# A two-layer encoder trunk on one core: the second layer's first projection taken from the unnormalised rows, and two steps of the feed-forward norm put in another order

## The chip, the cores and the metric

One core of one Trainium2 chip runs the whole kernel in one launch. The metric is the device time in microseconds (us) of that core. TensorE does the matmuls, VectorE (DVE in the rows) and ScalarE (ACT) the elementwise work, GpSimd (POOL) elementwise work beside them; SyncE (SP) issues every DMA.

## The reference, cut to what matters

The input is x (512 tokens by 1024 channels, float32) with a conditioning vector c. Two layers follow one another:

```
h   = modulated(LN(x))                 # scale and shift from c
z   = h @ w_in                         # 17 blocks of 128 columns
y   = four mixers(z) -> RMS per group -> @ w_out
x   = LN1(alpha * x + gate1 * y)
a   = conv3(modulated(x) @ w_up)       # 2 * 2816 columns, causal, width 3
x   = LN2(alpha * x + gate2 * ((val * silu(gate)) @ w_down))
```

The mixers are a gated MLP over 128 positions, latent attention, a diagonal state-space model (S5) and a gated linear recurrence (HGRN2). LN subtracts the mean over the 1024 channels and divides by the deviation.

## The kernel before

All activations lie channels by tokens: xa is 8 slices (k = 0 to 7) of 128 channels by 512 tokens and holds the residual stream, hm the modulated input. Weights come in chunks of 512 KB (128 by 1024) in a ring of 4 slots; SP loads a chunk when TensorE has begun one of the chunks before it (semaphore chunk_used). Every order is written out by hand, one list per engine, and semaphores tie the lists together.

There are five norms. Norm 1 is at the start; norms 2 and 4 stand between the output projection and the feed-forward part of layers 0 and 1; norm 3 stands between the layers and norm 5 at the end. A norm goes like this. VectorE adds each finished output bank to xa (residual, L1126) and adds up the slices (sum_x, L1134); ScalarE squares them (L1744); GpSimd adds the squares (L2078, L2210). TensorE multiplies the sums by a column of ones (norm_stats, L480: 32 records of 128x1). VectorE works out mean and variance on 4 columns (norm_var, L1069 to L1073), ScalarE the root (L1749), VectorE the reciprocal and the product mean * rstd (norm_rstd, L1078, L1080). TensorE spreads these two rows over the partitions (norm_spread, L475, 16 records) and VectorE applies them slice by slice (norm_apply: L1090 multiplies, L1096 subtracts). GpSimd then writes the modulated slice (modulate, L2090), and ScalarE turns xa into the next residual (affine, L1761).

In norms 2 and 4 the first block of w_up is already multiplied with the raw xa while the norm is worked out (raw_slice, L983, two records for a product). Since LN is linear in the rows but for mean and deviation, `up_raw` is put right afterwards: times the spread deviation, minus the column sums of the weighed weights times mean * rstd, plus a bias. The weights are weighed by weigh (L1648, two products), their column sums come from collect (L1654 to L1656, three additions of 1024, 512 and 256 columns with a wait after each of the first two) and from two small matmuls (L1000) before raw_slice(7). The other blocks of w_up are float32 matmuls in three parts (L460, L461, L462) from a high and a low half: ScalarE writes the high half of the weights (L1784), GpSimd the low half (weights_low, L2179), VectorE and GpSimd in turn the low half of the activations (h_low, L1669 for even k, L2219 for odd k). Blocks 1 and 2 go slice by slice with these (the pair loop), blocks 3 to 43 follow.

Between the layers (norm 3) there is no such raw product. TensorE does norm_pause: the sums, one filler matmul (keep_awake, L499), the spreads, two fillers. Then blocks CQ0 and CQ1 of w_in go slice by slice as hm comes in (L740), and CKV, F0, F1 and the rest follow by project (L551, two records for a product of 128x512), mixed with the mixers' small matmuls in a fixed order. At the same time VectorE goes from norm_apply straight to the mixers' tables: L1196 to L1202, then, after ScalarE's exponentials L1794 and L1795 (which stand behind the eight L1761), the S5 chain L1205 to L1326, and later the softmax of the attention (L1363), whose result TensorE turns at L713.

Of the kernel before, what the change touches and what calls it, by code (L numbers as in the profile page):

```python
# [13 lines left out]
P = 128  # L14
# [96 lines left out]
RAW_WEIGHED, RAW_SUM, RAW_UP, NRAW = 1, 2, 3, 3  # L111
# [28 lines left out]
def trunk(nc, x, consts, c_row, par_a, par_b, w_ada, w_in, w_out, w_up, w_down, out):  # L140
    ctx = ExitStack()
    with ctx:
# [128 lines left out]


# [4 lines left out]
        def sems(*names):  # L277
# [10 lines left out]
            **sems("silu_ready", "ada_used", "ln_par", "ln_sq", "ln_sumx", "ln_sumq", "ln_stat", "ln_var", "ln_sd",  # L288
                   "ln_rstd", "ln_bcast", "ln_normed", "ln_x", "ln_accx", "ln_accq", "h_par", "h_ready", "resid_mm", "resid"),
# [73 lines left out]
        def _(sp):  # L363
# [79 lines left out]
        def _(pe):  # L443
# [81 lines left out]
            last.then_inc(S["ln_accx"], 1)  # L525
# [5 lines left out]
            for l in range(L):  # L531

                def project(p, part):
# [15 lines left out]
                    else:  # L549
                        for k in ((0, 1, 2), (3, 4, 5), (6, 7))[part]:  # L550
                            last = mm(bank[:, :], w[:, k, :], hm[:, k, :], start=(k == 0), stop=(k == KD - 1))  # L551
                            if k == 0:
                                last.then_inc(S["chunk_used"], 2 if p == 2 else 1)
# [182 lines left out]
                w0, w1 = chunk(l, 0), chunk(l, 1)  # L736
                for k in range(KD):
                    pe.wait_ge(S["h_ready"], (2 * l) * KD + (k + 1))
                    for j, w in ((0, w0), (1, w1)):
                        last = mm(banks[2 + j][:, :], w[:, k, :], hm[:, k, :], start=(k == 0), stop=(k == KD - 1))  # L740
                        if k == 0 and j == 0:
# [265 lines left out]
                for k in range(KD):  # L1007
                    pe.wait_ge(S["h_lo_odd" if k % 2 else "h_lo"], l * (KD // 2) + k // 2 + 1)
                    for r, (w_hi, w_lo) in enumerate(pair):
# [4 lines left out]
                        if k == KD - 1:  # L1014
                            last.then_inc(S["up_mm"], 1)
                for m in range(3, 2 * KF):
# [38 lines left out]
                mm(banks[7][:, 63:64], ones, ones[:, 0:1], start=True, stop=True).then_inc(S["chunk_used"], TAIL - 1)  # L1055
                norm_pause(2 * l + 3, DOWN_DONE[-1])
# [3 lines left out]
        def _(v):  # L1060
# [21 lines left out]
            def norm_apply(n, low=None):  # L1082

                v.wait_ge(S["ln_bcast"], (n - 1) * 2 + 1)
                own = KD - SHARED if n == 2 * L + 1 else KD
                for k in range(own + (3 if low is not None else 1)):
                    if k == 5 and low is not None:
                        v.wait_ge(S["up_mm"], (n // 2 - 1) * (2 * KF) + 1)
                    if k < own:
                        ch.post(V.tensor_tensor(xa[:, k, :], xa[:, k, :], banks[0][:, :], ALU.mult))  # L1090
                    if k == 1:
                        v.wait_ge(S["ln_bcast"], (n - 1) * 2 + 2)
                    if 0 < k <= own:
                        if k == own:
                            ch.settle()
                        V.tensor_tensor(xa[:, k - 1, :], xa[:, k - 1, :], banks[1][:, :], ALU.subtract)\  # L1096
# [71 lines left out]
            v.wait_ge(S["silu_ready"], 1)  # L1168
# [17 lines left out]
            for l in range(L):  # L1186
# [486 lines left out]
                norm_rstd(2 * l + 2)  # L1673
                collect()
                norm_apply(2 * l + 2, h_low)

                v.wait_ge(S["up_mm"], l * (2 * KF) + 1)
# [48 lines left out]
                if l + 1 < L:  # L1726
                    modulated(l + 1, 0)
                for n, m in enumerate(DOWN_DONE):
                    residual(2 * l + 1, n, m, banks[m][:, :], g2p)
                    sum_x(2 * l + 1, n, DOWN_DONE)  # L1730
                norm(2 * l + 3)
                V.memset(small[:, 94:95], 0.0).then_inc(S["layer_done"], 1)
# [3 lines left out]
        def _(a):  # L1736
# [28 lines left out]
            A(silu_c[:, :], silu_c[:, :], ACT.Silu).then_inc(S["silu_ready"], 1)  # L1765
# [5 lines left out]
            a.wait_ge(S["ln_accx"], 1)  # L1771
# [14 lines left out]
            for l in range(L):  # L1786
# [21 lines left out]
                def evict(p):  # L1808
                    j = WIN[p]
                    a.wait_ge(S["proj_mm"], l * NPROJ + p + 1)  # L1810
                    bank = banks[2 + p] if p < 2 else banks[p % 2]
# [248 lines left out]
                if l + 1 == L:  # L2060
                    for r in range(2):
                        a.wait_ge(S["ln_bcast"], (2 * L) * 2 + 3 + r)
                        A(last_rows[:, r, :], banks[2 + r][:, :], ACT.Identity).then_inc(S["h_hi"], 1)
                affine(2 * l + 3, l + 1 < L)
# [3 lines left out]
        def _(g):  # L2068
# [28 lines left out]
            for l in range(L):  # L2097
# [123 lines left out]

                weights_low(KD + 3)
# [122 lines left out]
```

## Time and profile before

| | |
|---|---|
| median of 3 runs | 1423.6 us (1423.28 to 1427.83) |
| the profiled execution: its time, its span | 1428.15 us, 1426.4 us |
| TensorE busy | 1353.4 us, 95% of the span |
| VectorE, GpSimd, ScalarE busy | 785.5, 535.0, 506.2 us |
| mean granted TensorE clock | 0.966 of full |
| chain that ended last: TensorE, VectorE | 76%, 16% |

A busy TensorE is not one at its peak: a matmul's record overlaps the next one, and the rate is read from starts. Durations below are from this one execution.

### The profile page before, as it was taken

The page shows a single profiled execution, that of the slowest core. Times are in us where ns is not written, and L with a number is a line of the kernel's source. Part 1 is how long each engine was busy: PE and PEld are TensorE (multiplying, and loading weights), DVE is VectorE, ACT ScalarE, POOL GpSimd, SP SyncE. Part 2 cuts the span into 40 slices and gives each one's busy share as a digit, 9 for nine tenths or more (in the row PEclk, how much of TensorE's full clock was granted, in tenths as well). Part 3 has the DMA queues.
Part 4 walks back from the last instruction along what each step waited for, and adds up shares of the span by engine and source line. Part 5 has one row for each costly group of instructions (what it writes and reads, how often), then busy time and mean ns, then how long its engine had stood idle before and what let it go on. Part 6 is the DMA issues. An engine that isn't in the chain of part 4 may idle for free.

```text
span 1426.4 us, 17232 instructions
## 1 busy us (share of the span) xinstructions
PE 1353.4 (95%) x6868; PEld 1006.5 (71%) x6868; DVE 785.5 (55%) x1380; ACT 506.2 (35%) x766; POOL 535.0 (38%) x327
## 2 busy tenths in 40 slices
PE   6999999999999999899899999999999999989987
PEld 3445676786788888688665577677688888868866
DVE  5985778656776776432468656664743333321134
ACT  2523224335433333332242422442453333332223
POOL 0630100665444444344346110055644444434433
PEclk9998999999999999899999999999999999999998
DMA  9355733032555655454224451102133323223321
GB/s 385 146 118 163 170 121 100 16 103 89 188 196 190 188 182 180 160 178 161 106 72 112 84 74 37 45 17 84 49 103 98 95 89 102 90 74 89 97 66 60
DMA packets 64801, 166.79 MB, mean 117 GB/s; under 512 B 14288, under 2 KB 26960, under 8 KB 64208
## 3 DMA queue, kind: packets, MB, share of 16 engines
q1 hardware_dynamic: 64720, 165.68, 38.1%
q8 instruction: 55, 0.90, 0.2%
q14 instruction: 26, 0.21, 0.0%
HBM read 160.04 MB, written 5.62 MB: 116 GB/s over the span
## 4 chain that ended last, share of the span: by engine, by line
PE 76%; DVE 16%; issue 3%; DMA 2%; ACT 2%; POOL 1%; SPq 1%; ACTq 0%; POOLq 0%
PE bank L460 19%; PE bank L462 18%; PE bank L461 18%; PE bank L551 6%; PE bank L545 3%; PE bank L576 2%; PE bank L475 1%; DVE xa L1090 1%; DVE scr L1289 1%; PE bank L480 1%; DVE xa L1096 1%; PE bank L704 1%; PE bank L469 1%; DVE ada L1151 1%; DMA s_w<-scr 1%
## 5 line engine op out<-in xcount | busy, mean ns | idle before, releaser
L2179 POOL TENSOR_TENSOR ring_r<-ring,scr_r 128x1024 fp32r<-128x1024 f32 x146 | 352.8, 2418 | 450.0 <-ACT scr_r L1784 449.6
L460 PE MATMUL bank<-ym_r,scr_r 128*128 128x512 f32 x688 | 274.0, 398 | 5.2 <-DVE hm_r L1669 3.5
L462 PE MATMUL bank<-hm_r,scr_r 128*128 128x512 f32 x688 | 273.1, 397 | 0.0
L461 PE MATMUL bank<-ym_r,ring_r 128*128 128x512 f32 x688 | 270.4, 393 | 0.0
L460 PE MATMUL bank<-scr_r 128*128 128x512 f32 x480 | 196.8, 410 | 29.5 <-issue 14.2
L461 PE MATMUL bank<-scr_r,ring_r 128*128 128x512 f32 x480 | 191.0, 398 | 0.0
L1697 DVE SCALAR_TENSOR_TENSOR scr<-bank,pb,scr 128x511 f32<-128x511 f32 x86 | 64.5, 750 | 197.7 <-ACT scr L2035 197.6
L551 PE MATMUL bank<-hm,ring 128*128 128x512 f32 x352 | 171.0, 628 | 0.0
L1784 ACT ACTIVATE scr_r<-ring 128x1024 fp32r<-128x1024 f32 x146 | 152.7, 1047 | 39.9 <-DMA ring<-in_w_up 17.4
L1151 DVE SCALAR_TENSOR_TENSOR ada<-ada,silu_c 128x1024 f32<-128x1024 f32 x80 | 134.3, 1681 | 49.7 <-DMA ada<-in_w_ada 49.7
L460 PEld LDWEIGHTS bank<-ym_r,scr_r 128*128 128x128 f32 x688 | 129.3, 188 | 38.8 <-issue 5.1
L462 PEld LDWEIGHTS bank<-hm_r,scr_r 128*128 128x128 f32 x688 | 129.3, 188 | 32.2
L461 PEld LDWEIGHTS bank<-ym_r,ring_r 128*128 128x128 f32 x688 | 128.7, 187 | 32.3
L2035 ACT ACTIVATE scr<-bank,pb 128x512 f32<-128x512 f32 x86 | 66.7, 776 | 211.7 <-PE bank L462 211.7
L462 PE MATMUL bank<-scr_r 128*128 128x512 f32 x352 | 141.7, 403 | 0.0
L460 PEld LDWEIGHTS bank<-scr_r 128*128 128x128 f32 x480 | 92.7, 193 | 53.1 <-issue 16.3
L551 PEld LDWEIGHTS bank<-hm,ring 128*128 128x128 f32 x352 | 67.2, 200 | 73.2 <-issue 71.1
L461 PEld LDWEIGHTS bank<-scr_r,ring_r 128*128 128x128 f32 x480 | 92.9, 193 | 21.9
L1715 DVE TENSOR_TENSOR scr_r<-scr,scr_r 128x512 fp32r<-128x512 f32 x44 | 41.3, 939 | 121.5 <-ACT scr_r L2048 121.4
L462 PEld LDWEIGHTS bank<-scr_r 128*128 128x128 f32 x352 | 67.6, 192 | 18.6
L2048 ACT ACTIVATE scr_r<-scr 128x512 fp32r<-128x512 f32 x44 | 27.5, 628 | 145.0 <-PE bank L462 145.0
L1700 DVE SCALAR_TENSOR_TENSOR scr<-bank,pb,scr 128x510 f32<-128x510 f32 x86 | 64.4, 749 | 3.0
(351 smaller groups left out, 1762.4 us busy)
## 6 DMA issues: line engine op xcount, KB each, us to landing
ring<-in_w_up SPq DMA_DIRECT2D x88, 512.0 KB, 3.7
ada<-in_w_ada SPq DMA_DIRECT2D x80, 512.0 KB, 3.7
ring<-in_w_down SPq DMA_DIRECT2D x44, 512.0 KB, 3.6
ring<-in_w_in SPq DMA_DIRECT2D x34, 512.0 KB, 4.9
scr<-in_w_ada SPq DMA_DIRECT2D x16, 512.0 KB, 14.4
ring<-in_w_out SPq DMA_DIRECT2D x16, 512.0 KB, 3.7
pa<-in_par_a SPq DMA_DIRECT2D x2, 2144.5 KB, 12.9
xa<-in_x SPq DMA_DIRECT2D x1, 2048.0 KB, 8.2
```

Source lines behind the costliest of these rows:

```text
L460: first = mm(dst, w_hi, x_hi, start=start, stop=False)
L461: mm(dst, w_lo, x_hi, start=False, stop=False)
L462: return first, mm(dst, w_hi, x_lo, start=False, stop=stop)
L545: last = mm(bank[:, b * P:(b + 1) * P], hm[:, k, b * P:(b + 1) * P], w[:, k, :], start=(k == 0), stop=(k == KD - 1))
L551: last = mm(bank[:, :], w[:, k, :], hm[:, k, :], start=(k == 0), stop=(k == KD - 1))
L1151: V.scalar_tensor_tensor(ada[:, slot, :], ada[:, slot, :], 1.0, silu_c[:, :], ALU.mult, ALU.mult, accum_out=mods[:, MOD_PRE + i:MOD_PRE + ...
L1697: V.scalar_tensor_tensor(dst[:, 1:T], bank[:, 0:T - 1], pb[:, bass.ds(m * 3 + (o + 1), 1)], dst[:, 1:T], ALU.mult, ALU.add).then_inc(S["up ...
L1700: V.scalar_tensor_tensor(dst[:, 2:T], bank[:, 0:T - 2], pb[:, bass.ds(m * 3 + o, 1)], dst[:, 2:T], ALU.mult, ALU.add).then_inc(S["up_conv" ...
L1715: V.tensor_tensor(f_lo, hf[:, k, :], f_hi.bitcast(F32), ALU.subtract).then_inc(S["f_lo"], 1)
L1784: A(high[:, slot(l, n), :], ring[:, slot(l, n), :], ACT.Identity).then_inc(S["w_hi"], 2 if q == KD + 1 else 1)
L2035: A(cv[:, r, :], banks[2 + r][:, :] if m else up_raw, ACT.Identity, scale=pb[:, bass.ds(m * 3 + (o + 2), 1)], bias=pb[:, bass.ds(m + ob, 1 ...
L2179: G.tensor_tensor(ring_r[:, at, :], ring[:, at, :], high[:, at, :].bitcast(F32), ALU.subtract)\
```

## The change

**Between the layers.** The weights of CQ0 of layer 1 are loaded into a place of their own (next_w) as soon as the last low half of layer 0's feed-forward part is written. VectorE weighs them (2 products of 128x1024) and adds their columns up (3 additions) ahead of the eight residual additions. TensorE multiplies them with the raw xa in eight steps (next_slice): two before norm_stats, three between it and norm_spread, three after, with the two column matmuls before the last. The three fillers go. The spreads go to banks 5 and 6. norm_apply waits at k = 4 for the last raw slice. ScalarE copies the raw bank out before its affine; VectorE corrects it in four instructions behind norm_apply. In layer 1 the pair is then CQ1 with CKV, and CKV's own project goes.

**In norms 2 and 4.** GpSimd's weights_low(KD + 3) waits until both results of norm_rstd exist. collect moves behind norm_apply; its two column matmuls move behind the pair loop, and VectorE's correction waits for them.

```
@@ SP: load
+                if l and n == 0:
+                    sp.wait_ge(S["f_lo"], l * KF)
+                    sp.dma_start(next_w, w_in[l, j]).then_inc(landed[slot(l, n)], 16)
+                    return
@@ TensorE: the pair at the head of a layer
-                w0, w1 = chunk(l, 0), chunk(l, 1)
+                at = 0 if l == 0 else 1
+                w0, w1 = chunk(l, at), chunk(l, at + 1)
...
-                for part in range(3):
-                    project(AT[CKV], part)
+                if l == 0:
+                    for part in range(3):
+                        project(AT[CKV], part)
@@ TensorE: norms 2 and 4
                 raw_slice(6)
-                pe.wait_ge(S["raw_step"], l * NRAW + RAW_SUM)
-                for x in range(2):
-                    mm(banks[7][:, 72 + x:73 + x], columns[:, x, :], ones[:, 0:1], start=True, stop=True)
                 raw_slice(7)
... (the pair loop)
+                pe.wait_ge(S["raw_step"], l * NRAW + RAW_SUM)
+                for x in range(2):
+                    last = mm(banks[7][:, 72 + x:73 + x], columns[:, x, :], ones[:, 0:1], start=True, stop=True)
+                last.then_inc(S["accx_then_col"], 1)
@@ TensorE: end of a layer
-                mm(banks[7][:, 63:64], ones, ones[:, 0:1], start=True, stop=True).then_inc(S["chunk_used"], TAIL - 1)
-                norm_pause(2 * l + 3, DOWN_DONE[-1])
+                mm(banks[7][:, 63:64], ones, ones[:, 0:1], start=True, stop=True)\
+                    .then_inc(S["chunk_used"], TAIL if l + 1 < L else TAIL - 1)
+                if l + 1 == L:
+                    norm_pause(2 * l + 3, DOWN_DONE[-1])
+                else:
+                    pe.wait_ge(S["raw_step"], l * NRAW + NEXT + RAW_SUM)
+                    pe.wait_ge(S["resid"], (2 * l + 1) * KD + 4)
...
+                    next_slice(0)
+                    next_slice(1)
+                    norm_stats(2 * l + 3, DOWN_DONE[-1])
+                    next_slice(2)
+                    next_slice(3)
+                    next_slice(4)
+                    norm_spread(2 * l + 3, 5)
+                    next_slice(5)
+                    next_slice(6)
+                    for x in range(2):
+                        mm(banks[7][:, 72 + x:73 + x], next_columns[:, x, :], ones[:, 0:1], start=True, stop=True)
+                    next_slice(7)
@@ VectorE: norm_apply
+                    if k == 4 and ahead:
+                        v.wait_ge(S["proj_mm"], (n // 2) * NPROJ + 1)
@@ VectorE: norms 2 and 4
-                collect()
                 norm_apply(2 * l + 2, h_low)
-                v.wait_ge(S["up_mm"], l * (2 * KF) + 1)
+                collect()
+                v.wait_ge(S["accx_then_col"], l + 2)
@@ VectorE: between the layers, ahead of the residuals
+                    v.wait_ge(landed[slot(l + 1, 0)], landings(l + 1, 0))
+                    for x in range(2):
+                        ins = V.tensor_tensor(next_weighed[:, x, :, :], ..., ALU.mult)
+                    ... (three additions into next_columns)
@@ VectorE: behind norm 3
+                    v.wait_ge(S["proj_mm"], (l + 1) * NPROJ + 1)
+                    ch.post(V.tensor_scalar(st[:, 20:21], banks[7][:, 72:73], -1.0, None, ALU.mult))
+                    ch.post(V.tensor_scalar(st[:, 21:22], banks[7][:, 73:74], 1.0, None, ALU.mult))
+                    v.wait_ge(S["silu_then_raw"], l + 2)
+                    ch.post(V.tensor_tensor(next_raw, next_raw, banks[5][:, :], ALU.mult))
+                    ch.settle()
+                    V.scalar_tensor_tensor(next_raw, banks[6][:, :], st[:, 20:21], next_raw, ALU.mult, ALU.add)
@@ ScalarE: between norm 3's root and its affine; then the block's eviction
+                    a.wait_ge(S["proj_mm"], (l + 1) * NPROJ + 1)
+                    A(next_raw, banks[2][:, :], ACT.Identity).then_inc(S["silu_then_raw"], 1)
@@ GpSimd
+                g.wait_ge(S["ln_rstd"], (2 * l + 2) * 2)
                 weights_low(KD + 3)
                 modulate(2 * l + 2, 1, h_low)
```

## Rows read from the trace of the kernel before

**Rows 1.** Timeline of TensorE from norm 3 on: start, us, records, [idle before <- releaser].
```profile
720.71 1.93 PE L480 MATMUL bank<-cf,scr 128*128 128x1 f32 x16
...
725.78 3.67 PE L475 MATMUL bank<-cf,st 128*128 128x128 f32 x16 [0.40 <-DVE st L1078]
...
731.27 13.97 PE L740 MATMUL bank<-hm,ring 128*128 128x512 f32 x32
745.08 12.18 PE L551 MATMUL bank<-hm,ring 128*128 128x512 f32 x28
...
805.50 0.33 PE L713 MATMUL bank<-cf,scr 128*128 128x128 f32 x1 [1.34 <-DVE scr L1363]
```

**Rows 2.** Chain that ended last, 690 to 860: start, us, what.
```profile
739.89 1.28 ACT L1794
...
805.16 0.30 DVE scr L1363
```

**Rows 3.** Timeline of VectorE around norm 3.
```profile
700.45 0.76 DVE L1126 SCALAR_TENSOR_TENSOR xa<-bank,g2p,xa 128x512 f32<-128x512 f32 x1 [0.56 <-PE bank L462]
...
729.49 0.69 DVE L1096 TENSOR_TENSOR xa<-xa,bank 128x512 f32<-128x512 f32 x1 [0.18 <-PE bank L475]
...
737.87 0.35 DVE L1196 TENSOR_TENSOR small<-pa 128x2 f32<-128x2 f32 x1
...
741.63 0.29 DVE L1205 TENSOR_TENSOR scr<-scr,pa 128x128 f32<-128x128 f32 x1 [2.28 <-ACT small L1795]
```

**Rows 4.** Timeline of TensorE in norm 2 and after it.
```profile
325.90 4.52 PE L983 MATMUL bank<-xa,scr 128*128 128x512 f32 x6
330.26 1.95 PE L475 MATMUL bank<-cf,st 128*128 128x128 f32 x16
...
337.00 0.47 PE L460 MATMUL bank<-ym_r,scr_r 128*128 128x512 f32 x1 [1.78 <-DVE hm_r L1669]
...
345.22 0.50 PE L460 MATMUL bank<-ym_r,scr_r 128*128 128x512 f32 x1
...
367.25 0.50 PE L460 MATMUL bank<-ym_r,scr_r 128*128 128x512 f32 x1 [0.77 <-POOL ring_r L2179]
```

**Rows 5.** Windows: stretch, us, busy us (records) of PE, PEld, DVE, ACT, POOL; granted clock, DMA.
```profile
326.40:329.80 3.40, 3.40 (x5) 1.33 (x4) 3.02 (x6) 1.44 (x2) 2.34 (x1) 0.50 0.00 0
...
699.00:702.00 3.00, 3.00 (x8) 2.33 (x9) 1.52 (x6) 0.63 (x1) 0.00 (x0) 0.52 0.03 5
...
725.80:729.20 3.40, 3.40 (x16) 3.40 (x17) 1.39 (x3) 0.00 (x0) 0.00 (x0) 0.50 0.14 57
...
1031.00:1050.00 19.00, 18.86 (x81) 15.05 (x81) 11.05 (x18) 15.83 (x21) 9.48 (x6) 1.00 0.34 108
```

**Rows 6.** Timeline of VectorE in norm 2.
```profile
326.54 2.24 DVE L1072 TENSOR_TENSOR st<-st 128x4 f32<-128x4 f32 x1
...
329.55 1.22 DVE L1654 TENSOR_TENSOR scr<-scr 128x1024 f32<-128x1024 f32 x1
...
331.87 1.40 DVE L1090 TENSOR_TENSOR xa<-xa,bank 128x512 f32<-128x512 f32 x2
...
344.01 1.71 DVE L1669 TENSOR_TENSOR hm_r<-hm,ym_r 128x512 fp32r<-128x512 f32 x1 [0.15 <-POOL hm L2090]
...
346.48 0.75 DVE L1683 SCALAR_TENSOR_TENSOR scr<-bank,st,scr 128x512 f32<-128x512 f32 x1
```

**Rows 7.** Timeline of GpSimd in norm 2.
```profile
345.16 1.21 POOL L2090 TENSOR_SCALAR hm<-xa,gh 128x512 f32<-128x512 f32 x1
346.51 1.31 POOL L2219 TENSOR_TENSOR hm_r<-hm,ym_r 128x512 fp32r<-128x512 f32 x1
347.79 2.42 POOL L2179 TENSOR_TENSOR ring_r<-ring,scr_r 128x1024 fp32r<-128x1024 f32 x1
```

**Rows 8.** Timeline of ScalarE in norm 2.
```profile
326.36 1.28 ACT L1749 ACT_TABLE_LOAD   x1
...
351.21 0.71 ACT L2034 ACTIVATE scr<-scr,st 128x512 f32<-128x512 f32 x1
```

More of the change, by code:

```diff
@@ L552, in project @@
                             if k == 0:
-                                last.then_inc(S["chunk_used"], 2 if p == 2 else 1)
+                                last.then_inc(S["chunk_used"], 2 if p == (2 if l == 0 else 3) else 1)
                     if part == 2:
@@ L1054, in _, with next_slice @@
                 pe.wait_ge(S["resid"], (2 * l + 1) * KD + 1)
-                mm(banks[7][:, 63:64], ones, ones[:, 0:1], start=True, stop=True).then_inc(S["chunk_used"], TAIL - 1)
-                norm_pause(2 * l + 3, DOWN_DONE[-1])
+                mm(banks[7][:, 63:64], ones, ones[:, 0:1], start=True, stop=True)\
[5 more added lines that the diff above has]
+                    pe.wait_ge(S["resid"], (2 * l + 1) * KD + 4)
+                    def next_slice(i):
+                        pe.wait_ge(S["resid"], (2 * l + 1) * KD + i + 1)
+                        k = DOWN_DONE[i]
+                        last = mm(banks[2][:, :], next_weighed[:, 0, k, :], xa[:, k, :], start=(i == 0), stop=(i == KD - 1))
+                        if i == KD - 1:
+                            last.then_inc(S["proj_mm"], 1)
+                    next_slice(0)
[10 more added lines that the diff above has]
+                    next_slice(7)
         @block.vector
@@ L1085, in norm_apply @@
                 own = KD - SHARED if n == 2 * L + 1 else KD
+                ahead = low is None and 1 < n <= 2 * L - 1
+                factor, offset = (banks[5], banks[6]) if ahead else (banks[0], banks[1])
                 for k in range(own + (3 if low is not None else 1)):
@@ L1095, in norm_apply @@
                             ch.settle()
-                        V.tensor_tensor(xa[:, k - 1, :], xa[:, k - 1, :], banks[1][:, :], ALU.subtract)\
+                        V.tensor_tensor(xa[:, k - 1, :], xa[:, k - 1, :], offset[:, :], ALU.subtract)\
                             .then_inc(S["ln_normed"], 1)
@@ L1731, in _ @@
                 norm(2 * l + 3)
+                if l + 1 < L:
+                    v.wait_ge(S["proj_mm"], (l + 1) * NPROJ + 1)
[4 more added lines that the diff above has]
+                    ch.settle()
+                    V.scalar_tensor_tensor(next_raw, banks[6][:, :], st[:, 20:21], next_raw, ALU.mult, ALU.add)\
+                        .then_inc(S["raw_step"], 1)
                 V.memset(small[:, 94:95], 0.0).then_inc(S["layer_done"], 1)
@@ L1810, in evict @@
                     a.wait_ge(S["proj_mm"], l * NPROJ + p + 1)
-                    bank = banks[2 + p] if p < 2 else banks[p % 2]
+                    bank = banks[2 + p] if p < (2 if l == 0 else 3) else banks[p % 2]
+                    if l and p == 0:
+                        a.wait_ge(S["raw_step"], (l - 1) * NRAW + NEXT + RAW_UP)
+                        A(cq[0:QH, 0, :], next_raw[0:QH, :], ACT.Identity, bias=st[0:QH, 21:22])
+                        A(kro[NOPE:QK, 0, :], next_raw[QH:P, :], ACT.Identity, bias=st[QH:P, 21:22]).then_inc(S["proj_out"], 1)
+                        return
                     tok = bank[:, :].rearrange("p (b n) -> p b n", n=P)
```

39 lines of the change are left out of this document (28 added, 11 removed).

## The prediction

> **What bounds the kernel now.** I read the page first: TensorE is busy for 95% of the span, and the chain that ended last is 76% TensorE and 16% VectorE. That invites the reading that work taken from TensorE is time gained. So the second view is the chain around the place of the change. Behind norm 3 it is not on TensorE: it goes from the last apply through ScalarE's affine to the table load at 739.89, and then along VectorE's S5 tables and softmax to L1363 at 805.16 [rows 2]. TensorE joins at 805.50, after waiting 1.34 us for exactly that L1363 [rows 1]. From 731 to 805 TensorE is full of records, but it is only just late enough to hide that VectorE sets the end. The third view is the timelines of the norms, engine by engine. In norm 2 the reader is to see three things: one 4-column VectorE instruction that takes 2.24 us (L1072), because GpSimd's subtraction is running [rows 6]; TensorE's three raw slices between the sums and the spreads, which take 4.36 us, from 325.90 to 330.26 [rows 4]; and GpSimd's row of two-input work from 345.16 to 350.2 [rows 7]. Norm 4 shows the same pattern to within 0.1 us, 686 us later. After norm 4 TensorE alone is the bound (18.86 of 19.00 us busy [rows 5]); after norm 2 it is tied with ScalarE's eviction chain from 351.21 [rows 8], through GpSimd, to TensorE at 367.25, where TensorE has idled 0.77 [rows 4].
>
> **Norm 3, the raw projection.** Every time is in the profiled execution's span (1426.4 us; its own time was 1428.15, 4.5 above the median of the runs shown; I add the differences to the median, 1423.6).
>
> *Ahead of it.* The load is issued at about 698.8 and lands in some 4 us. Then VectorE weighs (2 x 1.22 by L1654, which has the same 1024 columns [rows 6]) and adds (1.22 + 0.7 + 0.4). The first residual moves from 700.45 [rows 3] to about 707.3. The banks come every 2.8 us (12 records at 0.233, the rate of 81 records in 18.86 us [rows 5]), and VectorE and GpSimd need about 2 us a step together, so the 7 us are made up by the seventh bank. Cost 0; if not made up, at most 1 to 2 us, of which the later sums hide 1.75.
>
> *The pause.* Two raw slices stand ahead of the sums: 4 records at 0.437 (32 in 13.97 [rows 1]), 1.75 us. The sums are bound by TensorE itself, 3.6 us. Then three slices, the spreads, three slices and two column matmuls. What the first three slices and the spreads take I read from norm 2, which has the same order: from 325.90 to 332.0, 6.1 us [rows 4]. Before, in norm 3, filler and spreads took from 724.3 to 729.3, 5.0 us [rows 1]. So the spreads are there 1.75 + 1.1 = 2.9 us later, and so is VectorE's first subtraction (729.49 [rows 3]). The wait at k = 4 costs nothing more: slices 5 to 7 and the columns take 3.1 us behind the spreads, which is when VectorE gets to k = 4.
>
> *Behind it.* GpSimd and ScalarE follow the apply, so the affine ends 2.9 later and the table load moves from 739.89 to 742.8. VectorE's four correcting instructions (about 1.6 us, as in norm 2, where L1683 at 346.48 is the last [rows 6]) and L1196 to L1202 lie inside the 2.28 us in which VectorE waited for ScalarE, with 0.6 to spare, since they grow from 1.5 to 3.1 and the gap was 3.8 from 737.87 to 741.63 [rows 3]. ScalarE's copy of the bank (0.6) is made up in the affine, which waits 0.38 a slice for GpSimd now. Thus L1205 and all behind it on VectorE come 2.9 us later, and nothing in that chain waited for TensorE.
>
> *What it saves.* TensorE loses 7 us of CKV's time behind the pair and gets 4.1 more ahead of it: it is 2.9 us ahead at F0. At 805.5 it waits for L1363 all the same, about 7 us instead of 1.3 there and at the gaps before. Term: **+2.9**. Bounds: -2.9, if TensorE were the bound after all, and +2.9 + 1.7, if the longer idling halves the clock at 806.
>
> TensorE's clock was half for 3.4 us in norm 3's spreads and in norm 2's slices, and TensorE was busy all that time (granted 0.50 [rows 5]); ahead of each stand only the one-column sums. Beside that stands a rule: the Trainium skill, "TensorE: Matmul & The Clock Gate", section "What's actually happening", ties the half clock to an idle TensorE; by it these stretches would run at full clock, and the term would be 1.2 instead of 2.9. The trace disagrees, and I take the rows.
>
> **Norms 2 and 4, GpSimd held.** L1072 falls from 2.24 to the 0.16 of its neighbours. Not all of it counts: ScalarE's table load lasts to 327.64 [rows 8], so the root comes 1.35 us earlier, not 2.08. And of that TensorE can use nothing, for its slices run until 330.26 at half clock either way [rows 4]. Bound: up to 1.3 a norm, in an execution in which the half clock falls elsewhere. GpSimd's subtraction now runs from 328.3 to 330.7, ahead of the apply; nothing is queued behind it that is due sooner. Cost 0.
>
> **collect out of the way.** Before, the three additions fill the time from 329.55 to 331.9, and the first multiplication starts at 331.87 [rows 6]. The first spread row is ready at about 331.3. Gain 0.55 us for the apply and all that follows it. Bounds 0.5 to 0.7.
>
> **collect behind the apply.** This is the dear part. The additions read two SBUF tiles, like L1669, which took 1.71 instead of 0.68 beside GpSimd [rows 6]. They now start at 345.2 and meet GpSimd's L2090, L2219 and L2179, one right behind the other [rows 7]; each addition waits for the one before, so each loses its turn to one GpSimd instruction. Written out with the 0.55 taken off: L2090 to 345.9; first addition to 347.0; L2219 (held back 1.1) to 348.25; second addition to 348.9; L2179 (2.35 us) to 351.2; third addition to 351.6. TensorE's pair loop had its last six records behind L2219; it ended at about 349.45 (18 records behind 345.22 [rows 4]) and ends at 349.7 now. It then waits for the third addition until 351.6 and does two column matmuls, 0.45. Block 3 starts at 352.05 instead of 349.45: **+2.6**. Before, the two column matmuls lay in TensorE's idle 1.78 ahead of 337.00 [rows 4] and cost nothing. VectorE's correction ends at 353.8, so ScalarE's L2034 moves from 351.21 to 353.85: the chain that set 367.25 is late by 2.6 as well, so layer 0 pays it on either path. Layer 1 pays it on TensorE's. Bounds of one norm: -0.1, where all additions slip through unhindered (-0.55 and +0.45), and +2.6; a halved clock behind the stall adds up to 1.7. I take the upper value, since the row that is nearest (L1669 beside the same GpSimd instructions) shows the full wait.
>
> **Sum.** 2.9 + 2.6 + 2.6 = 8.1: 1423.6 + 8.1 = 1431.7 us, 0.57% slower.
>
> **Rivals.**
>
> *The additions slip through.* For it: VectorE gets its turn between GpSimd instructions, and if L2179 comes a little later, the third addition is through by 349. Then each norm costs -0.1 to +1, and with norm 3's 2.9 the sum is +2.7 to +4: about 1427. It decides at the second addition: it has to end before L2179 is issued. Against: L2179 is ready at once behind L2219 in the rows.
>
> *TensorE's own queue decides (the other side).* If VectorE's chain behind norm 3 had more than the 1.34 us of slack, or the 16 spread records and slices fell in full clock, TensorE would carry its 2.9 us through, and with the holds worth 1.3 + 0.55 in each norm and free additions the sum is -2.9 - 2 x 1.4 = -5.7: 1417.9. It decides at 805: L1363 has to end before 802.3. Against: the chain of waits has no TensorE piece from 739.89 to 805.16.
>
> *Half clock on top.* The stall behind the pair, about 2 us behind another 0.8, and 7 us of gaps before 806, each followed by TensorE at half speed, as it was from 699 to 702 (0.52), where it had just waited for the last chunk of w_down [rows 5]. 1.7 us each, three places: +8.1 + 3 to 5 = 1436.
>
> *It does nothing.* The added waits are hidden by slack that I don't see: 1423.6. I find no such slack.
>
> **How the numbers follow.** Forecast 0.50; half clock on top 0.14; additions slip through 0.19; no effect 0.04; the other side 0.13. What a measurement of this kernel can tell from no change is 0.3%, 4.3 us. Slower: the first two and a fifth of the third, 0.68. Faster 0.12; same 0.20. The range reaches down to the slipping case and somewhat below it, and up to the half clock: 1422.5 to 1437. The likeliest case alone spans 1428.5 to 1434.
>
> **What would show it.** (1) L713 behind norm 3 starts 2.9 us later counted from the end of layer 0's last bank, with TensorE idling several us between 750 and it; were it earlier, the chain reading is wrong. (2) L1072 takes 0.16 and the root 0.2 right behind the table load, but the spreads still start some 4.4 us behind the sums. (3) L1656 ends about 2 us behind the pair loop in both layers, with L2179 between L1655 and L1656; TensorE idles until then. If it ends before the pair, that term is gone and I am 5 us too high. (4) The first residual of layer 0's end is about 7 us late and the last one is not. (5) The granted clock at the stall and at 806.

## The result, and the profile after

| | before | after |
|---|---|---|
| median of 20 runs each | 1424.14 us (1422.89 to 1431.84) | 1431.37 us (1422.73 to 1436.34) |
| ratio after to before, 95% interval | | 1.0038, 1.0025 to 1.0051 |
| profiled execution: time, span | 1428.15, 1426.4 us | 1429.77, 1428.0 us |
| mean granted TensorE clock of it | 0.966 | 0.970 |

The change costs 0.38%, which is 5.4 us (3.6 to 7.3). The forecast was 8.1 us; the direction and the range held. The ratio and the difference of the medians (7.2) are not the same, since executions of one kernel differ by up to 13.6 us here; the ratio is used below. That the median after (1431.37) lies beside the 1431.7 of the forecast is luck: the kernel before had a median of 1424.14 in these runs, not 1423.6, and by the ratio the forecast is 2.7 us too high. Two executions in the experiments below, one of the kernel before with 4744 us and one with GpSimd held with 3407 us, stand far outside all others and are left out of the ratios.

The two profiled spans differ by only 1.6 us, so they can't carry the argument. A part of the reason is the clock, which in these traces is either full or half: at a mean of 0.970 the execution after was at half clock for 2 x (1 - 0.970) x 1428 = 86 us, the one before for 2 x (1 - 0.966) x 1426 = 97 us. I therefore compare stretches that begin and end at the same events. "Sums end" is the start of the TensorE record that follows the 32 records of norm_stats. "The way" runs from layer 0's last output bank (the two 128x1 records that follow it on TensorE) to the turn of the softmax result; TensorE's idle time in it is the sum of the gaps that its timeline lists.

| us | before | after |
|---|---|---|
| norm 2: sums end to reciprocal / spreads / first multiplication of the apply | 3.35 / 4.36 / 5.97 | 2.03 / 4.36 / 5.45 |
| norm 2: sums end to block 3 on TensorE | 23.62 | 24.60 |
| norm 2: sums end to ScalarE's first correction copy | 25.31 | 26.50 |
| the way, and TensorE's idle time in it | 84.93, 3.50 | 88.07, 6.83 |

The page of the kernel after, its first and fourth part:

```profile
PE 1349.3 (94%) x6866; PEld 1002.3 (70%) x6866; DVE 793.2 (56%) x1389; ACT 506.9 (36%) x767; POOL 538.5 (38%) x327
...
PE 76%; DVE 15%; issue 3%; POOL 2%; DMA 2%; ACT 1%; SPq 1%; ACTq 0%; POOLq 0%
```

TensorE's busy time fell by 4.1 us, from 95 to 94% of the span, while the kernel got longer. That is no work saved: its records are as many as before (6866 and 6868), and it spent some 10 us less at half clock. Where the time went is seen in the stretches, first at norm 3. TensorE's timeline there, kernel after (it answers to [rows 1]):

```profile
717.12 0.28 PE L1069 MATMUL bank<-cf 128*128 128x1 f32 x2
717.26 1.96 PE L1081 MATMUL bank<-xa,scr 128*128 128x512 f32 x4
...
722.55 4.19 PE L1081 MATMUL bank<-xa,scr 128*128 128x512 f32 x6
726.53 2.30 PE L486 MATMUL bank<-cf,st 128*128 128x128 f32 x16
...
805.19 0.33 PE L724 MATMUL bank<-cf,scr 128*128 128x128 f32 x1 [1.34 <-DVE scr L1407]
805.36 4.44 PE L562 MATMUL bank<-hm,ring 128*128 128x512 f32 x6
```

Between the last bank and the spreads there are 9.41 us (717.12 to 726.53) with ten records of the raw slices among them; in the kernel before there are 5.22. VectorE's timeline, kernel after (it answers to [rows 3]):

```profile
697.75 2.36 DVE L1774 TENSOR_TENSOR scr<-scr,gh 128x1024 f32<-128x1024 f32 x2 [2.55 <-DMA scr<-in_w_in]
700.14 1.22 DVE L1778 TENSOR_TENSOR scr<-scr 128x1024 f32<-128x1024 f32 x1
...
702.47 1.41 DVE L1170 SCALAR_TENSOR_TENSOR xa<-bank,g2p,xa 128x512 f32<-128x512 f32 x2
...
714.59 0.75 DVE L1170 SCALAR_TENSOR_TENSOR xa<-bank,g2p,xa 128x512 f32<-128x512 f32 x1 [1.33 <-PE bank L473]
...
727.98 1.41 DVE L1134 TENSOR_TENSOR xa<-xa,bank 128x512 f32<-128x512 f32 x2 [3.78 <-PE bank L486]
...
738.52 0.75 DVE L1794 SCALAR_TENSOR_TENSOR scr<-bank,st,scr 128x512 f32<-128x512 f32 x1
...
741.44 0.29 DVE L1249 TENSOR_TENSOR scr<-scr,pa 128x128 f32<-128x128 f32 x1 [1.08 <-ACT small L1859]
```

The first residual stands 14.65 us ahead of the last bank instead of 20.12, 5.5 late; from the fifth bank on VectorE waits for TensorE again (0.82, then 1.33 at the sixth and seventh), so nothing of it is left. The S5 chain begins (L1249, before L1205) 24.32 us behind the last bank instead of 21.06: 3.26 late. VectorE's wait for ScalarE shrank from 2.28 to 1.08, since the correction (L1794 is its last instruction) lies in it.

The chain that ended last, kernel after, 690 to 860 (it answers to [rows 2]):

```profile
737.26 0.78 POOL hm L2162
738.12 0.70 ACT xa L1825
738.91 0.79 issue
739.70 1.28 ACT L1858
...
799.23 1.30 DVE scr L1524 x2
805.52 4.27 PE bank L562 x6
```

From the table load at 739.70 to 805 it holds no TensorE piece, as before. It is not VectorE's alone, though: a transfer of the attention's scratch (s_w) stands in it with 5.38 us, with 5.55 in the kernel before. Norm 2, in three timelines of the kernel after. VectorE (it answers to [rows 6]):

```profile
321.14 0.16 DVE L1112 TENSOR_TENSOR st<-st 128x4 f32<-128x4 f32 x1
...
322.53 0.18 DVE L1118 RECIPROCAL st<-st 128x4 f32<-128x4 f32 x1 [1.02 <-ACT st L1813]
...
338.11 1.70 DVE L1713 TENSOR_TENSOR hm_r<-hm,ym_r 128x512 fp32r<-128x512 f32 x1 [0.16 <-POOL hm L2162]
339.74 1.21 DVE L1698 TENSOR_TENSOR scr<-scr 128x1024 f32<-128x1024 f32 x1
340.98 1.07 DVE L1699 TENSOR_TENSOR scr<-scr 128x512 f32<-128x512 f32 x1
342.09 1.38 DVE L1700 TENSOR_TENSOR scr<-scr 128x256 f32<-128x256 f32 x1
```

GpSimd (it answers to [rows 7]):

```profile
339.25 2.27 POOL L2162 TENSOR_SCALAR hm<-xa,gh 128x512 f32<-128x512 f32 x1
341.66 1.52 POOL L2291 TENSOR_TENSOR hm_r<-hm,ym_r 128x512 fp32r<-128x512 f32 x1
343.15 2.57 POOL L2251 TENSOR_TENSOR ring_r<-ring,scr_r 128x1024 fp32r<-128x1024 f32 x1
```

TensorE (it answers to [rows 4]):

```profile
343.24 0.50 PE L471 MATMUL bank<-ym_r,scr_r 128*128 128x512 f32 x1 [0.87 <-POOL hm_r L2291]
...
344.74 0.50 PE L1028 MATMUL bank<-cf,scr 128*128 128x1 f32 x4
345.10 0.48 PE L471 MATMUL bank<-ym_r,scr_r 128*128 128x512 f32 x1
```

The first addition (L1698) follows VectorE's last low half without a gap, and it is GpSimd's modulate (L2162) that waits: 2.27 us instead of 1.21. All three additions are through at 343.47, before the pair loop is (344.74). What TensorE waits for is GpSimd's last low half (L2291), 0.87 us, and then come the column matmuls, 0.36 from start to start. Norm 4 shows the same order: modulate 2.26, the additions 1.21, 1.06 and 1.38, block 3 at 24.58 us behind the sums' end (23.58 before).

### The profile page after: what moved, and what is told of

Same layout as the page of the kernel before. It is cut to its first block, busy times and chain, and to the rows that moved or that the text cites. A ratio compares the mean times of both kernels' runs of the same rounds, so it can differ in the third digit from the quotient of the medians.

```text
span 1428.0 us, 17244 instructions
## 1 busy us (share of the span) xinstructions
PE 1349.3 (94%) x6866; PEld 1002.3 (70%) x6866; DVE 793.2 (56%) x1389; ACT 506.9 (36%) x767; POOL 538.5 (38%) x327
## 4 chain that ended last, share of the span: by engine, by line
PE 76%; DVE 15%; issue 3%; POOL 2%; DMA 2%; ACT 1%; SPq 1%; ACTq 0%; POOLq 0%
PE bank L471 19%; PE bank L473 18%; PE bank L472 18%; PE bank L562 5%; PE bank L556 3%; PE bank L587 2%; PE bank L486 1%; DVE scr L1333 1%; DVE xa L1134 1%; PE bank L491 1%; DVE ada L1195 1%; DVE xa L1140 1%; POOL hm L2162 1%; PE bank L715 1%; PE bank L996 1%
## 5 line engine op out<-in xcount | busy, mean ns | idle before, releaser
L562 PE MATMUL bank<-hm,ring 128*128 128x512 f32 x336 | 162.5, 624 | 0.0
L562 PEld LDWEIGHTS bank<-hm,ring 128*128 128x128 f32 x336 | 63.4, 198 | 68.3 <-issue 66.1
```

## The experiments

The ratio is the kernel's time to that of the kernel before, run beside it (5 rounds, 12 runs of each kernel and 29 or 35 of the kernel before), with its 95% interval. With intervals of some 0.2% on either side a single norm of 1 us can't be told by time, so the verdicts rest on the stretches, and each stretch is from one execution. How far a stretch can be trusted is seen in the four kernels below that leave everything between the layers as it was: their way is 84.65 to 85.78 us long, where the kernel before has 84.93.

### Norm 3 alone, and the two norms alone

The edits are the halves of the change: in the one, norms 2 and 4 are as in the kernel before; in the other, everything between the layers is.

Norm 3 alone:

> Only the raw projection between the layers; norms 2 and 4 as before. Theory (VectorE's chain behind norm 3 sets the end): from the last output bank of layer 0 to the softmax result's turn on TensorE takes 3.0 us more than in the kernel before (84.9 us there), TensorE idles several us on the way, and the time is 3 us longer, 1.7 more where the clock halves at that turn. Rival (TensorE's queue decides): the same stretch is 2.9 us shorter.

Norms 2 and 4 alone:

> Only the two edits in norms 2 and 4 (GpSimd's subtraction held, collect behind the apply). As predicted before the result: 2.6 us more in each norm. As the changed kernel's trace now reads: the first two additions get through and GpSimd's last slice is late instead, 1.1 us more in each norm, 2.3 us in all. Rival: the hold's 2 us come through and the norms are shorter.

| | median | ratio | the way / idle | norm 2: reciprocal / apply / ScalarE |
|---|---|---|---|---|
| norm 3 alone | 1426.87 | 1.0010 (0.9991 to 1.0030) | 88.15 / 7.21 | 3.31 / 5.92 / 25.26 |
| norms 2 and 4 alone | 1426.40 | 1.0011 (0.9991 to 1.0030) | 85.57 / 2.84 | 2.01 / 5.27 / 26.30 |

The two halves separate in the stretches: the way grows by 3.2 us with norm 3's half, and in norm 2 ScalarE's correction comes 1.0 us later with the other. In norm 4 of that other kernel it came 0.5 us earlier than before (24.79 behind the sums' end, 25.28 before), since the slices ran at full clock there; the 1.1 us more in each norm were thus seen in one of the two. By time both are inconclusive, and their sum (3.0 us) lies below the 5.4 of the whole with intervals that reach over it. The runs with norms 2 and 4 alone had on average a somewhat higher clock (0.969) than those of the kernel before beside them (0.967), so their time shows the price of the edits less than fully.

### TensorE relieved behind norm 3

The rival on the other side had TensorE's queue as the bound of the way. This kernel is the one before with six of the eight slices of CKV's product left out in layer 1.

```
-                for part in range(3):
-                    project(AT[CKV], part)
+                if l == 0:
+                    for part in range(3):
+                        project(AT[CKV], part)
+                else:
+                    w = chunk(l, 2)
+                    mm(banks[0][:, :], w[:, 0, :], hm[:, 0, :], start=True, stop=False).then_inc(S["chunk_used"], 2)
+                    mm(banks[0][:, :], w[:, 7, :], hm[:, 7, :], start=False, stop=True).then_inc(S["proj_mm"], 1)
```

> The kernel before with six of the eight slices of CKV's product left out in layer 1 (its values are wrong there), so TensorE has 5.2 us less to do between norm 3 and the softmax, and no other engine has anything changed. Theory: the stretch from the last output bank to the turn of the softmax result keeps its 84.9 us, TensorE idles 5 us more on the way. Rival (TensorE bound): the stretch is up to 5 us shorter, less the 1.3 to 3 us of slack.

Measured: the way 84.87 us (84.93 before), TensorE's idle time in it 8.27 (3.50 before); 1426.42 us, ratio 1.0009 (0.9988 to 1.0030). TensorE's timeline in this kernel at the end of the way:

```profile
804.49 0.33 PE L713 MATMUL bank<-cf,scr 128*128 128x128 f32 x1 [1.34 <-DVE scr L1368]
804.65 1.88 PE L551 MATMUL bank<-hm,ring 128*128 128x512 f32 x4
```

Some 5 us of TensorE's work are gone, the idle time grows by 4.8, and the turn comes as before. Work taken from TensorE on the way behind norm 3 is worth nothing, which is why the 4 us that the change moves ahead of it could only cost.

### Fewer raw slices ahead of the spreads

Both kernels have norm 3's change alone and leave raw slices out: the first the two ahead of the sums, the second all five ahead of the spreads. The first slice that is left starts the sum in the bank. The second kernel's edit is shown, the first has only its two upper lines.

```
-                    next_slice(0)
-                    next_slice(1)
                     norm_stats(2 * l + 3, DOWN_DONE[-1])
-                    next_slice(2)
-                    next_slice(3)
-                    next_slice(4)
                     norm_spread(2 * l + 3, 5)
```

Two left out:

> Norm 3's change alone, with the two raw slices ahead of the sums left out of the product (the raw block sums six slices instead of eight, so its values differ). Theory: all that stands on TensorE ahead of the spreads delays VectorE one for one, so the way from layer 0's last output bank to the softmax result's turn is 88.15 - 1.75 = 86.4 us (88.15 with all eight slices), and the time about 1.7 us below norm 3's change alone. Rival: the first slices fill time in which the sums would wait for GpSimd's squares anyway; then the sums start no earlier, and the way stays at 88.1.

Five left out:

> Norm 3's change alone, with all five raw slices ahead of the spreads left out of the product (three slices are summed instead of eight). Theory: the spreads and the apply start as early as in the kernel before, which had fillers there, and VectorE's four correcting instructions stay hidden in its wait for ScalarE, so the way is 84.9 us and the time that of the kernel before. Rival: the load, the weighing and the additions ahead of the residuals, or the correction and the bank copy behind the apply, carry a part of the 3.1 us; then the way stays above 86.

Measured: two left out, the way 88.02, 1426.32 us, ratio 1.0006 (0.9990 to 1.0022); five left out, the way 84.85, 1424.75 us, ratio 1.0005 (0.9989 to 1.0021). The second is what the theory said. The first is not: the way is no shorter. The rival's reason is out as well, since the sums do start earlier (0.14 us behind the last bank instead of 1.94). The timeline and the windows tell what took the gain. TensorE's timeline, two slices left out:

```profile
720.30 1.93 PE L491 MATMUL bank<-cf,scr 128*128 128x1 f32 x16
722.09 1.71 PE L491 MATMUL bank<-cf,xa 128*128 128x1 f32 x8
723.66 1.84 PE L491 MATMUL bank<-cf,hm 128*128 128x1 f32 x8
725.37 4.66 PE L1080 MATMUL bank<-xa,scr 128*128 128x512 f32 x6
```

Its windows (columns as in [rows 5]):

```profile
720.30:723.30 3.00, 3.00 (x26) 3.00 (x24) 0.75 (x1) 0.63 (x1) 0.18 (x1) 0.83 0.60 158
723.30:726.30 3.00, 3.00 (x12) 2.55 (x12) 0.65 (x5) 0.00 (x0) 0.00 (x0) 0.50 0.90 366
726.30:729.80 3.50, 3.50 (x6) 1.47 (x5) 0.41 (x3) 0.20 (x1) 0.00 (x0) 0.60 0.00 0
```

In this execution the clock fell to half already in the sums (eight records in 1.71 and 1.84 us instead of 1.03) and stayed there through most of the slices. The sums took 5.07 us instead of 3.6, which takes back 1.5 of the 1.75 us spared, and the spreads start 9.70 us behind the last bank (9.78 with all slices). Whether the half clock would fall there in every execution is open.

With five left out, TensorE idles 1.37 ahead of the spreads, the apply starts 7.34 us behind the last bank (before 7.33), and VectorE's timeline shows the rest of the change hidden:

```profile
739.12 0.75 DVE L1789 SCALAR_TENSOR_TENSOR scr<-bank,st,scr 128x512 f32<-128x512 f32 x1
...
742.04 0.29 DVE L1243 TENSOR_TENSOR scr<-scr,pa 128x128 f32<-128x128 f32 x1 [1.09 <-ACT small L1854]
```

L1243 starts 21.12 us behind the last bank, against 21.06 before, with the load, the weighing, the additions, the bank copy and the correction all in. In the stretches the five slices ahead of the spreads are the whole of norm 3's price; by time the two kernels (1.0005 and 1.0010) can't be told apart.

### GpSimd held, in two ways

The hold alone, on the norm's two results as in the change, and on the column sums instead.

```
+                g.wait_ge(S["ln_rstd"], (2 * l + 2) * 2)
                 weights_low(KD + 3)
```

```
+                g.wait_ge(S["raw_step"], l * NRAW + RAW_SUM)
                 weights_low(KD + 3)
```

On the norm's results:

> Only the hold, collect stays ahead of the apply. Theory: the reciprocal is there 1.35 us earlier (table load), collect then ends about when the first spread row is there, so the apply starts 0.5 us earlier and each norm is 0.5 us shorter, not 2: the spreads still start 4.4 us behind the sums, bound by TensorE's three slices at half clock. Rival: the 2.1 us of the stalled instruction come off each norm, 4 us in all.

On the column sums:

> The kernel before, with GpSimd's subtraction held until the three additions are done (not only the reciprocal). Theory after the run with the hold alone, where the second addition sat 2.0 us behind that subtraction: the additions now end 4.6 us behind the sums, the apply starts at +5.45 instead of +5.95, and each norm is 0.5 us shorter up to ScalarE's correction (+24.8 instead of +25.3). Rival: the subtraction, now starting at about +4.7, delays the apply or the pair loop instead, and nothing is gained.

| sums end to ... in norm 2 | reciprocal | first multiplication | ScalarE's correction | median | ratio |
|---|---|---|---|---|---|
| before | 3.35 | 5.97 | 25.31 | | |
| held for the norm's results | 2.04 | 6.68 | 26.00 | 1430.64 | 1.0032 (1.0012 to 1.0052) |
| held for the column sums | 1.87 | 5.43 | 24.81 | 1424.18 | 0.9988 (0.9974 to 1.0003) |

The hold on the norm's results, without the move of collect, makes the apply 0.7 us later, in norm 2 as in norm 4 (6.58 instead of 5.93), where I had expected it 0.5 earlier. VectorE's timeline in that kernel:

```profile
328.87 1.22 DVE L1654 TENSOR_TENSOR scr<-scr 128x1024 f32<-128x1024 f32 x1
330.12 2.72 DVE L1655 TENSOR_TENSOR scr<-scr 128x512 f32<-128x512 f32 x1
```

GpSimd's timeline in the same kernel:

```profile
329.03 3.26 POOL L2179 TENSOR_TENSOR ring_r<-ring,scr_r 128x1024 fp32r<-128x1024 f32 x1 [5.93 <-DVE st L1080]
```

GpSimd is released just as the additions begin. It waits out the first and then holds the second, 2.72 us instead of 0.69. So in the whole change the two moves belong together: the hold needs collect out of the way. But the hold on the column sums reaches the same early apply (5.43) with collect where it was, and without the price behind the apply; ScalarE's correction comes 0.5 us earlier in both norms (24.81 and 24.83, before 25.31 and 25.28).

By time the hold on the norm's results costs 4.6 us (1.7 to 7.4), which is more than these 0.7 us a norm. In its profiled execution TensorE ran at half clock through a part of norm 2's pair loop, and block 3 came 25.90 us behind the sums' end instead of 23.62. Whether that explains the rest is open. The gain of the hold on the column sums is not shown by time (0.9988, 0.9974 to 1.0003).

### collect moved alone

```
                 norm_rstd(2 * l + 2)
-                collect()
                 norm_apply(2 * l + 2, h_low)
-                v.wait_ge(S["up_mm"], l * (2 * KF) + 1)
+                collect()
+                v.wait_ge(S["accx_then_col"], l + 2)
```

with the two column matmuls behind the pair loop.

> The kernel before, with collect and its two column matmuls behind the pair loop but without the hold. Theory: the reciprocal stays at +3.3 (the 4-column instruction stalls), the spreads stay at +4.36, the apply starts at +5.45, and behind it all is as in the run with both edits: 1.1 us more than before in each norm. So the hold contributes nothing where TensorE's slices run at half clock. Rival: without the hold the apply is later than +5.45.

Measured: 1427.05 us, ratio 1.0008 (0.9995 to 1.0021). In norm 2 the reciprocal comes at 3.30, the spreads at 4.36, the apply at 5.45, all as expected, and ScalarE's correction at 26.49 (25.31 before). GpSimd's timeline in this kernel:

```profile
345.06 2.26 POOL L2090 TENSOR_SCALAR hm<-xa,gh 128x512 f32<-128x512 f32 x1
347.47 1.52 POOL L2219 TENSOR_TENSOR hm_r<-hm,ym_r 128x512 fp32r<-128x512 f32 x1
```

The same 2.26 and 1.52 as after: the price of norm 2 is collect's, wholly. The hold in the change as made has no effect on it. In norm 4 of this execution the half clock began within the sums, the spreads came at 5.26 and the correction at 27.79, 1.3 us later than after (26.48); so the 1.1 us a norm were seen in norm 2 alone.

### The exponentials earlier

If the chain through ScalarE's table load sets the way, moving that load shortens it. In the kernel before, ScalarE issues L1794 and L1795 for layer 1 right behind norm 3's root, ahead of its eight affine copies, instead of behind them. For layer 0 they stay where they were.

```
                 norm(2 * l + 3)
+                if l + 1 < L:
+                    a.wait_ge(S["para_in"], 16 * (l + 1) + 16)
+                    A(W(0), p_a("s5_ls"), ACT.Exp)
+                    A(small[:, 24:32], p_a("s5_sls"), ACT.Exp).then_inc(S["s5_dt"], 1)
```

Alone:

> The kernel before, with ScalarE's two exponentials for layer 1's S5 tables (L1794, L1795) put between norm 3's root and its affine, where ScalarE idles 5.7 us, so that the table load leaves VectorE's chain. Theory (that chain sets the end): VectorE's 2.28 us of waiting go, and the stretch from the last output bank to the softmax result's turn falls from 84.9 to 82.7 us; TensorE's idling there falls from 3.5 to about 1.3. Rival (TensorE bound): the stretch keeps its 84.9.

With GpSimd held for the column sums:

> Both of the two above. Theory: the sum of both, 3.2 us less than before: 2.2 between the layers and 0.5 in each of norms 2 and 4. Rival: no change beyond noise.

With both, and with norm 3's raw projection:

> Norm 3's raw projection together with the two edits that shortened the kernel before: GpSimd held in norms 2 and 4 until the column sums exist, and the exponentials of the S5 part issued in layer 0's norm 4 part, so that their table load lies in ScalarE's idle time. Theory: with the raw projection VectorE waits only 1.1 us for the exponentials, so the early ones give 1.1 instead of 1.9: the way from the last bank to the turn is about 87.1, 4 us longer than the same two edits give without the raw projection (83.1 to 83.9), and the time some 3 to 4 us above theirs. Rival: with the exponentials gone from the way TensorE becomes the bound behind norm 3, the raw projection pays, and the way falls to 83 or below.

(The exponentials stand where the lines above show, behind norm 3's root.)

| | the way / idle | median | ratio |
|---|---|---|---|
| exponentials early | 83.07 / 2.15 | 1426.67 | 0.9997 (0.9979 to 1.0015) |
| and held for the column sums | 83.93 / 1.68 | 1421.68 | 0.9976 (0.9957 to 0.9995) |
| and the raw projection | 88.62 / 7.62 | 1423.84 | 0.9990 (0.9976 to 1.0005) |

ScalarE's timeline, exponentials early:

```profile
725.00 0.20 ACT L1749 ACTIVATE st<-st 128x4 f32<-128x4 f32 x1 [3.14 <-DVE st L1073]
725.23 1.28 ACT L2062 ACT_TABLE_LOAD   x1
...
730.94 0.81 ACT L1761 ACTIVATE xa<-xa,ga 128x512 f32<-128x512 f32 x1 [4.01 <-POOL hm L2094]
...
739.49 0.19 ACT L1797 ACTIVATE small<-small 128x4 f32<-128x4 f32 x1
```

The load of 1.28 us now lies in an idle time of 4 us, the affine copies and L1797 behind it need no other, and the way is 1.86 us shorter (2.2 expected); TensorE idles 2.15 us in it, where I expected 1.3. It is shorter than in any kernel that leaves this stretch alone (84.65 at the least). By time the exponentials alone show nothing (0.9997, 0.9979 to 1.0015).

With GpSimd held for the column sums as well, the time is 3.4 us below the kernel before (0.7 to 6.1), the lowest here; 3.2 were expected. In its profiled execution the parts are the way, 1.0 shorter, and ScalarE's correction, 0.5 earlier in norm 2 and 1.35 in norm 4, where the slices ran at full clock.

With the raw projection in, the S5 chain starts 23.28 us behind the last bank instead of 24.34 (norm 3 alone): the 1.06 that the theory gives. The turn was to be at 87.1 and was at 88.62, because one transfer of the attention's scratch took longer. The chain of that kernel:

```profile
769.22 6.95 DMA s_w<-scr
```

In norm 3 alone the same piece takes 5.43, and in the kernel before 5.55. Why it took 1.5 more in this one execution the trace does not show. The rival is refuted all the same: TensorE idles 7.62 us, so even without the table load it is not the bound, and the raw projection does not pay. By time this kernel lies some 2 us above the one without the raw projection (ratios 0.9990 and 0.9976), where 3 to 4 were expected; the two intervals overlap.

## Why the prediction was right or wrong

**What bounds the kernel.** Right, and shown for the way: relieving TensorE left it as long as it was, and moving one table load on ScalarE shortened it.

**Norm 3, +2.9.** Right in mechanism and nearly in size: the way grew by 3.14 (after) and 3.22 (norm 3 alone). *Ahead of it* cost 0, as said; the first residual was 5.5 us late (7.1 in norm 3 alone; I had 7), and the last not at all. *The pause* carries all of it, as the kernel without the five slices shows. *Behind it*, the correction stayed in VectorE's wait, with 1.08 to spare where I had 0.6. *What it saves*: TensorE's idle time on the way grew by 3.3, from 3.5 to 6.8, in the gaps before the turn; at the turn itself it idles 1.34 as before. I had more, about 7 instead of 1.3; in this execution TensorE ran one more group of matmuls at half clock on the way (eight records of the attention at 774.52 took 5.37 us instead of 3.60).

**Norms 2 and 4, GpSimd held, 0.** Right for the forecast: L1112 takes 0.16, the reciprocal comes 1.3 us earlier, and the spreads start at 4.36 us as before, because the half-clock slices fill the time. The bound of up to 1.3 a norm was seen too, and somewhat more than it: in norms 2 and 4 alone the half clock did not fall on norm 4's slices, the spreads started at 2.66 and the apply at 3.75 instead of 5.93.

**collect out of the way, -0.55.** Right for what it was priced on: the apply started 0.52 us earlier. What I missed is that the two edits are tied: with the hold as made and collect left in place it is +0.7.

**collect behind the apply.** This is the step that failed, a term of the wrong size: right that the price lies here, but too high. I summed +2.6 a norm; up to block 3 it is +0.98 in norm 2 (23.62 to 24.60) and +1.00 in norm 4 (23.58 to 24.58), up to ScalarE's correction 1.2 in both. The error is the order of the turns. I let GpSimd's modulate come first and each addition lose one turn to a GpSimd instruction. In the rows L1698 starts right behind VectorE's own L1713 and modulate loses the turn; only the third addition (1.38 instead of 0.42) and, in part, the second (1.07 instead of 0.69) wait. So the additions end at 22.97 us, before the pair and not 2 us behind it, and the stall is GpSimd's instead: modulate +1.06 and low half +0.21, less the 0.52 gained, make it 0.75 late, TensorE ends the pair 0.62 later, and 0.36 of column matmuls follow. The same order stands in both norms of all three kernels that move collect. This is the upper end of the rival in which the additions slip through (-0.1 to +1 a norm), but for another reason: they slip through at GpSimd's expense. That rival's sum was added up wrongly, too: 2.9 + 2 x 1 is 4.9 and not 4, and the measured 5.4 lies nearer to it than to the forecast's 8.1. The sign that I gave (additions ended before the pair: 5 us too high) came true in the rows, but the norms still paid 1 us each, and the forecast was 2.7 too high.

**Sum.** 3.14 + 0.98 + 1.00 = 5.1 us against 5.4 (3.6 to 7.3) measured; predicted 8.1. So close an agreement is in part luck: the way differs by 1.1 us between executions of kernels that are alike there, and by time the two halves of the change sum to 3.0 us only.

**The rivals.** *The other side* (TensorE's queue decides) is refuted by the shortened CKV. *No effect* is refuted by the ratio. *Half clock on top*: it does come behind the turn, where I named it, but not in every execution, and not at the stall behind the pair. In the profiled one after, six records behind the turn took 4.27 us of the chain instead of 2.58. Windows, kernel after:

```profile
321.10:324.50 3.40, 3.40 (x6) 1.32 (x5) 0.68 (x5) 1.38 (x2) 1.52 (x1) 0.50 0.00 0
...
805.80:809.20 3.40, 3.40 (x6) 1.34 (x4) 1.76 (x5) 0.62 (x3) 0.00 (x0) 0.50 0.17 63
```

It is no term of the change, since the kernel with early exponentials has it too (4.44 us for those six records in its timeline) and norm 3 alone doesn't (2.74). Such stretches go with the spread of 9 to 13.6 us between executions of one kernel: of the 20 runs after, the fastest (1422.73 us) had a mean clock of 0.977 and the slowest (1436.34) one of 0.965. The Trainium skill ("TensorE: Matmul & The Clock Gate", section "What's actually happening") ties the half clock to an idle TensorE. The second of these rows has 1.34 us of idling ahead of the turn, but so has the kernel before, where the same matmuls ran at full clock; the first does not go with the rule, since TensorE was busy without a gap ahead of it, with raw slices and one-column matmuls. In norm 3 of the kernel before, other than I wrote, the sums are not all that stands ahead of the spreads: a filler and 0.40 us of idling lie between.

## What to carry to other kernels

Before work is moved ahead of a norm to fill a TensorE that looks idle there, follow the chain behind the norm. Here it ran over VectorE and ScalarE; what was put ahead of the spreads was paid, 3.1 us for five slices that stood where the kernel before had a filler and a short wait, and what it saved on TensorE became idle time. A helper sum did better in a gap of its own engine, with the other engine held until it was done (0.5 us earlier in each norm), than moved behind the engine's main work (1.0 us later). A cheap gain lay on the chain itself: a table load placed in ScalarE's idle time made it 1.9 us shorter. The kernel with that hold and this load together is the only one here that its time shows to be faster.

## What the runs showed of the hardware that was not expected

When VectorE and GpSimd each have an instruction ready, one can hold the other up for its whole length. In the kernel after, GpSimd's L2162 was held from 1.21 to 2.27 us by L1698, which itself took its 1.21. In the kernel with the hold alone it was the other way round: L1655, which waits for the addition before it, lost its turn and took 2.72 us instead of 0.69, ending 0.55 behind GpSimd's L2179. The Trainium skill ("SBUF — State Buffer", section "🔬 SBUF: two separate sides") says that where a VectorE instruction has two SBUF inputs and a GpSimd one reads SBUF, whichever of the two starts first holds the shared pair of ports for its whole instruction. These rows agree with it in that the loser waits the other out. In who wins they don't, if a start is that of the record: L2162's stands at 339.25, ahead of L1698's 339.74, and yet L1698 was not held up.

Who gets the next turn stays open. L1698 follows its predecessor on VectorE without a wait, which would be an explanation, but a little behind norm 3 of the same kernel L1267 does so too and loses to GpSimd's L2184 (from 743.66, 1.04 us), with 1.15 us instead of 0.28. VectorE's timeline, kernel after:

```profile
743.70 1.15 DVE L1267 TENSOR_TENSOR scr<-pa 128x128 f32<-128x128 f32 x1
```

The order of the turns made up the 1.6 us a norm by which the forecast was off.

The half clock can also fall on the one-column sums themselves: in the kernel with two slices left out they took 5.07 instead of 3.6 us, with the granted clock at 0.50 from 723.30 on and TensorE busy throughout.
